# Block 1's attention taken by pairs of heads in a three-block kernel on one core

## What is computed

```python
logits = einsum('bqhd,bqkhd->bhqk', qb, k_sel) * scale
logits = logits + bias                       # rel_bias by distance bucket
logits = where(valid, logits, -inf)
probs = softmax(logits, axis=-1)
return einsum('bhqk,bqkhd->bqhd', probs, v_sel)
```

## Time and profile before

| what | value |
|---|---|
| median of 3 runs (lowest, highest) | 3023.46 us (3020.39, 3025.13) |
| the profiled execution's own time | 3024.29 us |
| its span, first to last instruction | 3022.5 us |
| busy: PE, PEld | 2889.2 us (96%), 2296.4 us (76%) |
| busy: DVE, ACT, POOL | 1270.9 us (42%), 1147.1 us (38%), 1510.4 us (50%) |
| the attention's steps in the span | about 226 to 362 us |

### The profile page before, as it was taken

How to read it: one execution, slowest core, us unless ns; L and a number is a source line. 1 busy time by engine, 2 the same in 40 slices (tenths; PEclk the granted TensorE clock), 3 DMA queues, 4 the chain that set the end, 5 groups by cost and what they waited for, 6 DMA issues and landing times.

```text
span 3022.5 us, 41145 instructions
## 1 busy us (share of the span) xinstructions
PE 2889.2 (96%) x15600; PEld 2296.4 (76%) x15600; DVE 1270.9 (42%) x2023; ACT 1147.1 (38%) x1676; POOL 1510.4 (50%) x1883
## 2 busy tenths in 40 slices
PE   7999989899999999989999999989999988999998
PEld 6776668688888876768888888757777676888886
DVE  4066664553211745143362225151466733562222
ACT  4534633542222427234342225253444424442222
POOL 5345511456555665537665564514326324665653
PEclk9999999999999999999999999989999899999999
DMA  4322200333333433326322222312212104522222
GB/s 140 99 84 92 65 19 3 119 105 98 97 94 96 138 99 98 104 68 204 126 98 98 95 95 96 118 46 84 73 53 97 49 20 150 171 92 97 98 98 84
DMA packets 80673, 284.16 MB, mean 94 GB/s; under 512 B 8968, under 2 KB 9096, under 8 KB 79744
## 3 DMA queue, kind: packets, MB, share of 16 engines
q1 hardware_dynamic: 66240, 236.36, 24.4%
q10 hardware_dynamic: 13296, 41.97, 3.7%
q0 software_dynamic: 976, 3.56, 0.4%
HBM read 260.86 MB, written 20.99 MB: 93 GB/s over the span
## 4 chain that ended last, share of the span: by engine, by line
PE 43%; POOL 27%; issue 23%; DVE 3%; ACT 3%; POOLq 0%; DMA 0%; ACTq 0%; SPq 0%; DVEq 0%
POOL slab_r L3060 26%; PE bank L382 11%; PE bank L383 10%; PE bank L384 10%; PE bank L631 2%; PE bank L515 1%; PE bank L608 1%; PE bank L702 1%; PE bank L1085 1%; PE bank L525 1%; PE bank L750 1%; PE bank L1009 1%; PE bank L1114 0%; PE bank L813 0%; PE bank L689 0%
## 5 line engine op out<-in xcount | busy, mean ns | idle before, releaser
L3060 POOL TENSOR_TENSOR slab_r<-slab,slab_high 128x256 fp32r<-128x256 f32 x1768 | 1409.6, 829 | 1296.9 <-ACT slab_high L1259 1290.0
L382 PE MATMUL bank<-xh,slab_high 128*128 128x512 f32 x2256 | 904.0, 401 | 15.0 <-POOL slab_r L3060 14.9
L384 PE MATMUL bank<-xh,slab_r 128*128 128x512 f32 x2256 | 881.3, 391 | 0.0
L383 PE MATMUL bank<-x_raw_r,slab_high 128*128 128x512 f32 x2064 | 806.6, 391 | 0.0
L1259 ACT CAST slab_high<-slab 128x1024 fp32r<-128x1024 f32 x442 | 462.6, 1047 | 429.3 <-DMA slab<-in_w_down 209.6
L383 PE MATMUL bank<-work_r,slab_high 128*128 128x512 f32 x1376 | 536.9, 390 | 0.0
L382 PEld LDWEIGHTS bank<-xh,slab_high 128*128 128x128 f32 x2256 | 425.7, 189 | 133.2 <-issue 27.6
L384 PEld LDWEIGHTS bank<-xh,slab_r 128*128 128x128 f32 x2256 | 425.1, 188 | 90.3
L382 PE MATMUL bank<-work_r,slab_high 128*128 128x512 f32 x1184 | 465.8, 393 | 23.0 <-DMA cst<-in_cst 15.3
L384 PE MATMUL bank<-work_r,slab_r 128*128 128x512 f32 x1184 | 461.8, 390 | 0.0
L383 PEld LDWEIGHTS bank<-x_raw_r,slab_high 128*128 128x128 f32 x2064 | 389.7, 189 | 80.5 <-issue 3.6
(11 more groups left out here) (459 smaller groups left out, 2774.1 us busy)
## 6 DMA issues: line engine op xcount, KB each, us to landing
slab<-in_w_down SPq DMA_DIRECT2D x88, 512.0 KB, 3.5
slab<-in_w_up SPq DMA_DIRECT2D x64, 512.0 KB, 3.4
slab<-in_w_gates SPq DMA_DIRECT2D x56, 512.0 KB, 3.5
slab<-in_w_merge SPq DMA_DIRECT2D x48, 512.0 KB, 4.1
slab<-in_w_gu SPq DMA_DIRECT2D x44, 512.0 KB, 3.6
slab<-in_w_in_a SPq DMA_DIRECT2D x32, 512.0 KB, 3.6
gates<-staging ACTq DMA_DIRECT2D x56, 256.0 KB, 2.1
slab<-in_w_out SPq DMA_DIRECT2D x24, 512.0 KB, 3.5
```

Of the source, the lines that this page charges most:

```text
L382: first = pe.matmul(bank[b][:, :], wh, mh, start=start, stop=False)
L383: pe.matmul(bank[b][:, :], wh, ml, start=False, stop=False)
L384: end = pe.matmul(bank[b][:, :], wl, mh, start=False, stop=stop)
L3060: low = pool.tensor_tensor(slab_low[:, slot, at], slab[:, slot, at], plain(slab_high[:, slot, at]), ALU.subtract)
```

## The change

Logits of two heads are issued together, two steps ahead: logits(0) and logits(1) before the attention, then logits(g+2) and logits(g+3) at each even step. Values are taken for two heads at once at each even step g (pair g/2 - 1), their instructions alternating between the two column halves (64 partitions) of bank 7, ahead of turn_probs(g); ScalarE copies both halves with one instruction of 128 partitions. Probabilities have four tiles (W(57), W(58), W(36), W(37)) instead of two. VectorE takes add_max(0) and add_max(1) first and then, in step g, scale_probs(g) before add_max(g+2). POOL's code and the order of its work are as before.

```diff
--- before.py
+++ after.py
@@ -340,6 +340,7 @@
         A_ALONE, A_SUMS, A_FLIPS, A_VALUES, A_SCORES = 8, range(9, 13), range(13, 17), (15, 16), range(18, 30)
         PICKS, PICKS_ALONE = TOPK // 8, 4
         SHIFT_FROM = 16
+        PROBS = (57, 58, 36, 37)
 
         GLA_STEPS = [(h, half) for h in range(4) for half in (256, 128, 64, 32, 16, 8, 4, 2, 1, 0)]
         WEIGHTS = (32, 45)
@@ -707,6 +708,7 @@
                 if p == 31:
                     mark("attention")
                     logits(0)
+                    logits(1)
                 slab_alone(p % RING)
                 if p == A_ALONE:
                     bias_table()
@@ -738,17 +740,19 @@
             def turn_probs(g):
                 i, h = steps[g]
                 pe.wait_ge(S("probs_ready"), n.next(S("probs_ready")))
-                turned[g] = turn([(W(57 + g % 2)[:, s * P:(s + 1) * P], s * P) for s in range(i + 1)], 6, "act")
-
-            def values(g):
-                i, h = steps[g]
-                r = slice(HD * (h % 2), HD * (h % 2) + HD)
-                pe.wait_ge(*turned[g])
+                turned[g] = turn([(W(PROBS[g % 4])[:, s * P:(s + 1) * P], s * P) for s in range(i + 1)], 6, "act")
+
+            def values(pair_no):
+
+                i, h0 = steps[2 * pair_no]
+                pe.wait_ge(*turned[2 * pair_no + 1])
                 if last[7]:
                     pe.wait_ge(*last[7])
                 for s in range(i + 1):
-                    ins = pe.matmul(bank[7][r, 0:P], W(48 + s)[:, h * HD:(h + 1) * HD],
-                                    W(59 + g % 2)[:, s * P:(s + 1) * P], start=(s == 0), stop=(s == i))
+                    for e in range(2):
+                        h = h0 + e
+                        ins = pe.matmul(bank[7][e * HD:(e + 1) * HD, 0:P], W(48 + s)[:, h * HD:(h + 1) * HD],
+                                        W(59 + e)[:, s * P:(s + 1) * P], start=(s == 0), stop=(s == i))
                 ins.then_inc(psum_for["act"], hand(7, "act"))
 
             def rates(c):
@@ -762,8 +766,9 @@
                         .then_inc(psum_for["act_beside"], hand(b, "act_beside"))
 
             for g in range(len(steps) + 1):
-                if g + 1 < len(steps):
-                    logits(g + 1)
+                if g % 2 == 0 and g + 2 < len(steps):
+                    logits(g + 2)
+                    logits(g + 3)
                 if g < len(steps):
                     early_gates(in_attention(g))
                     if g in RATES_AT:
@@ -771,9 +776,10 @@
                             pe.wait_ge(S("lora_ready"), n.next(S("lora_ready")))
                             pe.wait_ge(S("lora_loads"), n.next(S("lora_loads"), 48))
                         rates(RATES_AT.index(g))
+                if g % 2 == 0 and g:
+                    values(g // 2 - 1)
+                if g < len(steps):
                     turn_probs(g)
-                if g >= 1:
-                    values(g - 1)
 
 
             mark("key_sums")
@@ -1561,8 +1567,8 @@
                 i, h = steps[g]
                 b = g % 2
                 act.wait_ge(S("logits_ready"), n.next(S("logits_ready")))
-                act.activation(W(57 + b)[:, 0:(i + 1) * P], W(57 + b)[:, 0:(i + 1) * P], ACT.Exp, bias=SM(200 + b),
-                    accum_out=SM(204 + b))\
+                probs = W(PROBS[g % 4])[:, 0:(i + 1) * P]
+                act.activation(probs, probs, ACT.Exp, bias=SM(200 + b), accum_out=SM(204 + b))\
                     .then_inc(S("exps_ready"), n.up(S("exps_ready")))
                 act.wait_ge(S("exps_ready"), n.own(S("exps_ready")))
 
@@ -1573,11 +1579,11 @@
                 act.copy(W(59 + g % 2)[:, 0:(i + 1) * P], bank[6][:, 0:(i + 1) * P]).then_inc(evac, n.up(evac))
                 act.wait_ge(evac, n.own(evac))
 
-            def valued(g):
-                i, h = steps[g]
-                r = slice(HD * (h % 2), HD * (h % 2) + HD)
+            def valued(pair_no):
+
+                i, h = steps[2 * pair_no]
                 act.wait_ge(psum_for["act"], n.next(psum_for["act"]))
-                act.copy(W(32 + h // 2)[r, i * P:(i + 1) * P], bank[7][r, 0:P]).then_inc(evac, n.up(evac))
+                act.copy(W(32 + h // 2)[:, i * P:(i + 1) * P], bank[7][:, 0:P]).then_inc(evac, n.up(evac))
 
             def key_squares():
                 for c in range(4):
@@ -1594,7 +1600,7 @@
                     act.activation(W(o + c), bank[RATE_BANKS[c] + e][:, :], ACT.Sigmoid, bias=V(bias, c))\
                         .then_inc(by_beside, n.up(by_beside))
 
-            for g in range(len(steps) + 2):
+            for g in range(len(steps) + 1):
                 if g < len(steps):
                     exps(g)
                 if g == HIDDEN_AT:
@@ -1606,8 +1612,8 @@
                         rates(c)
                 if 1 <= g <= len(steps):
                     turned(g - 1)
-                if g >= 2:
-                    valued(g - 2)
+                if g % 2 == 0 and g:
+                    valued(g // 2 - 1)
                 if g == len(steps):
                     key_squares()
                 send_gates(in_attention(g) if g < len(steps) else 0)
@@ -2467,7 +2473,7 @@
                 w, b = (i + 1) * P, g % 2
                 dve.wait_ge(psum_for["dve"], n.next(psum_for["dve"]))
                 dve.wait_ge(S("bias_ready"), n.next(S("bias_ready")))
-                dve.tensor_tensor_reduce(out=W(57 + b)[:, 0:w], in0=bank[4 + b][:, 0:w], in1=W(55 + b)[:, 0:w],
+                dve.tensor_tensor_reduce(out=W(PROBS[g % 4])[:, 0:w], in0=bank[4 + b][:, 0:w], in1=W(55 + b)[:, 0:w],
                     scale=1.0, scalar=-3e+38, op0=ALU.add, op1=ALU.max, accum_out=SM(208 + b))\
                     .then_inc(evac, n.up(evac))
                 dve.wait_ge(evac, n.own(evac))
@@ -2481,14 +2487,16 @@
                 dve.wait_ge(S("exps_ready"), n.next(S("exps_ready")))
                 dve.reciprocal(SM(202 + b), SM(204 + b)).then_inc(chain, n.up(chain))
                 dve.wait_ge(chain, n.own(chain))
-                dve.tensor_scalar(W(57 + b)[:, 0:w], W(57 + b)[:, 0:w], SM(202 + b), None, ALU.mult)\
+                probs = W(PROBS[g % 4])[:, 0:w]
+                dve.tensor_scalar(probs, probs, SM(202 + b), None, ALU.mult)\
                     .then_inc(S("probs_ready"), n.up(S("probs_ready")))
 
             add_max(0)
+            add_max(1)
             for g in range(len(steps)):
-                if g + 1 < len(steps):
-                    add_max(g + 1)
                 scale_probs(g)
+                if g + 2 < len(steps):
+                    add_max(g + 2)
                 if picked[NT - 1] < PICKS:
                     top_k(NT - 1, 1)
```

## The result

| | before | after |
|---|---|---|
| median of the runs taken together (lowest, highest) | 3023.05 us (3020.39, 3025.13) | 3045.43 us (3043.93, 3046.92) |
| ratio after to before, 95% interval | | 1.0069 (1.0057 to 1.0081) |
| span of the profiled execution | 3022.5 us | 3044.9 us |
| shift 16 ends | 286.76 us | 292.64 us |
| shift 29 ends | 348.16 us | 364.56 us |

The forecast was 3026.5 us, with a range from 3016 to 3033. The kernel is slower by 0.69%, three and a half times the 0.2% that the prediction took as the least that can be told.

A forecast was written before the change was run, and what follows sets the result against it. TensorE was taken as full in the attention's second half, with a POOL-VectorE loop binding after the change. Terms -3.7 + 6.2 + 1.3 - 0.75 = +3.05 us on the 3023.46 us median gave 3026.5 us, range 3016 to 3033.

The forecast's parts named there:

- The pairs: TensorE in block 1's attention: a pair costs what one head costs, saving 22.9 us in all.
- The ring: Shift 16 to shift 29: a POOL, VectorE, POOL loop binds each turn, 67.6 us where 61.4 were taken before.
- Low parts: POOL's steps 19, 21, 24, 26 and 29: each adds 2.8 us to the loop, 14.1 us in sum.
- Contention with the scaling: Steps 17 to 29: VectorE's scale_probs meets POOL's shift difference, 0.1 us a turn, 1.3 us in all.
- What arrives at shift 16: Attention's first half: shift 16 ends 3.7 us early, within ±2.5, near 283.1 us.
- The saving of 8.0: TensorE up to step 16: pairs save 4.2 us of logits and 3.8 us of values.
- The stalls of 2.9 us in all: Steps 8 to 13: values copy ahead of exps and delayed low parts lose 2.9 us of the early saving.
- The wait of shift 16 itself: Shift 16 comes 4.5 us after step 16 began instead of 3.1, bias(18) waiting for a low part: 1.4 us lost.
- The tail: Shift 29's end to the third scan group: 16.75 us instead of 17.5, 0.75 us gained.
- The whole sum: All terms: -3.7 + 6.2 + 1.3 - 0.75 = +3.05 us on the median, giving 3026.5 us.
- The clock falls: Rival: TensorE idles in the loop and drops to half clock, +10 to +15 us, 3034 to 3039; chance 0.03.
- The saving comes through: Rival: the loop has unseen slack and the pairs' saving arrives, -15 to -20 us, 3003 to 3008; chance 0.12.

The follow-up runs named there:

- e3: After, with POOL's biases made one step earlier and ScalarE's values copy moved to the odd step behind exps; ratio to before 0.9962, median 3013.30 us.
- e2: After, with ScalarE's values copy moved from the even step to the following odd step, behind its exps; ratio to before 1.0007, median 3029.95 us.
- e9: e7 with 69 more unused matmul products where TensorE stood idle in steps 17 to 29; ratio to before 1.0040, median 3038.47 us.
- e10: e2 with VectorE's scale_probs working on only 8 columns from step 17 on; ratio to before 1.0006, median 3025.72 us.
- e7: After, with eight unused matmul products added in TensorE's step 9 ahead of turn_probs; ratio to before 1.0040, median 3040.50 us.
- e1: After, with POOL making bias(g+2) in step g, ahead of the shift's difference; ratio to before 0.9998, median 3025.98 us.
- e6: e3 with POOL's bias(1) moved ahead of its wait for ScalarE and three DMA issues; ratio to before 0.9955, median 3013.02 us.
- e8: e6 with ScalarE's cast, gate copy and store right behind exps, ahead of the copies; ratio to before 0.9945, median 3011.43 us.
- e5: Before, with only the values pair and its even-step copy; logits, VectorE order and tiles as before; ratio to before 0.9998, median 3025.22 us.
- e4: Before, with logits two steps ahead, four probability tiles and VectorE's new order, but no pairs; ratio to before 1.0018, median 3031.30 us.

## Why the prediction was wrong, point by point

**The pairs (right).** 1.06 and 1.02 us for two heads at 512 columns. From 226 us to shift 29 TensorE was busy 122.15 us before (60.80 up to 286.8, 61.35 behind it), and 102.45 in e3. These 19.7 us are not all saved: e3 has 547 matmuls there and before has 559, since VectorE's shift 29 runs ahead; twelve products are some 2.8 us. That leaves some 17 us, with part of e3's at a low clock (0.83 over 310 to 320 us).

**The ring (right in mechanism and place, its size 3.0 us short).** The stretch was given as 67.6 + 1.3 = 68.9 us and took 71.92. Of the 3.0, 1.0 is the values copy and the low clock together, most of it in the last turn, 7.94 us: take either away and it goes, the copy in e2 (70.93, last turn 7.31, its own clock at 0.93), the low clock in e9 (71.11, 7.28). The turns without contention took 4.33 and 3.95 us (e10) where 4.28 and 3.86 were summed: the hand-over from bias to add_max is 0.14 and not 0.07. Over thirteen turns that is 0.85 us. Four of the wide turns (22 to 25, apart from their low part) took 4.51: VectorE's further instruction of steps 21 to 24 (L2505 before), named in the description and left out of the sum, runs beside the difference's first instruction (L3150), which takes 0.38 us in place of 0.21; 0.7 in all. Low parts cost 2.75 each and not 2.8, 0.3 the other way. Together 1.3: 68.91 measured in e10, 67.6 reckoned. Contention with the scaling is 2.0 us where 1.3 was taken: 0.7.

**What arrives at shift 16 (the step that failed).** Forecast 3.7 us early, measured 5.9 late: 9.6 of the 22 us. The saving of 8.0 was there: in e2 TensorE is busy 55.4 us up to shift 16 for 283 matmuls, before 60.8 for 271. The stalls of 2.9 us in all were wrong twice. First, the chain valued, cast, gate copy, exps was found and written down for step 8, yet priced as 1.15 us of idleness of TensorE; the idleness at 259.17 is 1.92. From the copy's start to the next exps it took 2.10 us, as forecast (2.09), but from there to turn_probs 2.18 and not 1.4; scale_probs took 0.87 of it, beside POOL's low part, and in the earlier trace rows 0.43. The queue behind the waiting copy (the cast, behind it POOL's low part, behind that the next bias) was seen too and given 0.7 us at step 10 and 0.4 and less at the later ones; in after POOL waited 30.0 us for casts in five waits. With the copy moved (e2) shift 16 comes at 282.50, 4.3 us early, near the forecast of 283.1. So what the copy's place costs up to there is 10.1 us, where the whole list of stalls had 2.9. Second, nothing in that list made TensorE slower after a stall; by e7 this was 4.3 of the 10.1 in the profiled execution, though e1 shows the same stall without it. The wait of shift 16 itself was nearly right: from step 16's logits (287.56) to its end 5.1 us, forecast 4.5. The late bias(1) at 227 us, 1.1 to 1.5 us (e6), was missed altogether, by reading only POOL's order in the loop and not the DMA issues ahead of it. Some of the 10.1 and the 8.7 that e1 gives is the same loss, for together they give 12.2 (e3).

**The tail (right at full clock, wrong as it came).** 16.75 us were summed; e9, with the clock kept up to 370 us, took 16.56. In after it took 19.0: the 2.4 us more went with the clock. The copy's place is in the sum: without it the tail is 14.9 (e2).

**The whole sum, and luck.** e2 is the kernel with the mis-sized step mended, and its scan comes at 368.30 where 368.7 was forecast for after. That is partly luck: counted from before, its parts are -4.3, +9.5 and -2.6 us where the sum had -3.7, +7.5 and -0.75.

**"The clock falls" (the rival at 3034 to 3039).** The nearest to the result, and given 3 in 100. It was set in the wrong place, though: I had it fall in the loop and cost there. It fell there too (0.91), at a cost of 0.8 us, since the ring and not TensorE set most of the time. It cost where TensorE was on the path: 4.3 us in the first half, behind a single stall, and 2.4 behind the loop. The row held against it (3.71 busy of 5 us at 1.00) was one stretch; after has 3.39 of 5 at 0.56. A busy share does not tell the clock: what came before the stretch counts as well. The Trainium skill, TensorE: Matmul & The Clock Gate, Part 1, lets the clock follow how busy the array has been of late; the traces here agree (0.50 at 262 to 266 us with TensorE busy all of it, behind the stall at 257 to 259 us).

**"The saving comes through".** Not in after. In e6 and e8, which undo the two waits, 0.45 to 0.55% comes through, 14 to 17 us of the 22.9, at the low end of what that rival had, 15 to 20.

**Left open: the 4.5 us behind the scan.** The same code from the third scan group to the end took 2656.9 us before and 2661.3 after, but also 2652.9 in e5, 2654.7 in e2, 2656.7 in e3, 2660.4 in e9 and e10 and 2665.4 in e7, kernels that don't differ there. The shortest has the highest mean clock over the whole span (e5, 0.981), the two longest the lowest (e7 0.971, after 0.973); no experiment ties after's 4.5 to the change. The medians have it too: 22.4 us, where the scan comes 17.9 later.

## What to carry to other kernels

When a step is moved on one engine, ask for each engine which instruction now waits with others queued behind it, and follow that queue, not only the wait: a 0.27 us copy ahead of cast and exps cost nearly as much as a ring through POOL and VectorE. Work taken from the full engine is only worth something once both the ring and the order behind it leave it full; the order alone (e4) and the pair alone (e5) each show a loss or nothing, and both mended with the pairs kept gain 0.4 to 0.55%. And when a busy TensorE is to be stalled for the first time, charge the stall, and count on slow matmuls behind it as a possibility with a price of its own.

## What the runs showed of the hardware

- In after, a stall of 1.92 us in a stretch that had been full was followed by a fall of TensorE's clock: 0.70 over 258 to 262 us, 0.50 (its lower level) over 262 to 266, 0.95 over 266 to 270; a product then cost 0.43 us in place of 0.23. Filling the gap with 1.98 us of useless matmuls kept 1.00 and brought later work 4.3 us forward. In e1 a stall of 1.93 us at the same place was followed by no fall (1.00 over 226 to 284 us).
- Where the clock is low and TensorE is mostly off the path, it costs little: the stretch was 71.11 us at 1.00 (e9), 71.92 at 0.91 (after) and 73.46 at 0.90 (e7), the last two with POOL waiting for a cast behind the values copy; with the copy out of the way it was 70.93 at 0.93 (e2).
- A VectorE scaling of 512 columns that begins 0.14 us ahead of a GpSimd difference of 511 lengthens the latter from 1.04 to 1.23 us. The other way round, a scaling of 8 columns that begins inside the difference takes 0.98 us in place of 0.23 (e10).
- Two groups of matmuls on different column halves that write one bank run side by side: 16 instructions in 1.02 us, the time of 8 of one head.
